# A decoder trunk on one core: the final sum as products with diagonal matrices, queries by halves of the tokens, output weights loaded during the merge

## The reference, cut to what matters

```python
x = layer_norm(x_in)                                  # D_MODEL = 1024
z = x @ w_in + b_in                                   # nine streams of 512 columns, four gates of 1024
mix = (sum over 4 branches of sigmoid(gate) * (branch @ w_branch)) @ w_out      # the merge, then w_out
x = layer_norm(ALPHA * x + mix)
x = layer_norm(ALPHA * x + cross_attend(x, mem))      # queries x @ x_wq, 4 heads, 256 memory rows, then @ x_wo
s = sigmoid(x @ router_w)                             # 16 experts; the best group of 4, the best 2 experts in it
h = silu(x @ e_wg[e]) * (x @ e_wu[e])                 # each expert on the tokens that chose it
y = sum over the two chosen experts of w[e] * (h @ e_wd[e])
out = layer_norm(ALPHA * x + y)
```

## Time and profile before

| what | value |
|---|---|
| runs | median 1628.93 us of 3 (1626.19 to 1635.36) |
| profiled execution: own time, span | 1631.28 us, 1629.5 us |
| PE busy | 1403.6 us (86%) |
| DVE, ACT, POOL busy | 752.3 us (46%), 538.4 us (33%), 239.5 us (15%) |
| mean granted TensorE clock | 0.938 of full speed |
| chain of waits, by engine | PE 37%, DMA 7%, DVE 4%, ACT 2%, SP's queue 2%, issue 2% |

### The profile page before, as it was taken

The page is one execution under the profiler, slowest core; times in us unless marked ns, Lnnn a source line. Parts: engine busy times, 40 slices in busy tenths (PEclk is TensorE's granted clock), DMA queues, the critical chain, the costliest instruction groups (busy, mean ns, idle before and its releaser), DMA issues.

```text
span 1629.5 us, 18477 instructions
## 1 busy us (share of the span) xinstructions
PE 1403.6 (86%) x7275; PEld 1166.8 (72%) x7275; DVE 752.3 (46%) x1079; ACT 538.4 (33%) x729; POOL 239.5 (15%) x211
## 2 busy tenths in 40 slices
PE   4989989899896688899999798987896799999940
PEld 4767868677685576798999686775684588887730
DVE  5024133242425546753111143032345699888847
ACT  1234421424312033421000001144201488777721
POOL 4200000000005422132333000001000110010023
PEclk9999999999997899999999998999997799999985
DMA  9613332331002222124222603126802699999941
GB/s 323 229 48 104 97 99 78 86 97 39 16 0 58 59 59 59 39 78 129 78 78 87 224 0 103 52 100 249 283 33 97 214 378 395 394 394 394 394 176 66
DMA packets 175091, 239.84 MB, mean 147 GB/s; under 512 B 6048, under 2 KB 108633, under 8 KB 174881
## 3 DMA queue, kind: packets, MB, share of 16 engines
q1 hardware_dynamic: 156896, 181.13, 32.9%
q0 software_dynamic: 14832, 52.57, 9.1%
q10 hardware_dynamic: 3281, 5.00, 1.0%
HBM read 214.08 MB, written 24.60 MB: 146 GB/s over the span
## 4 chain that ended last, share of the span: by engine, by line
PE 37%; DMA 7%; DVE 4%; ACT 2%; SPq 2%; issue 2%; POOL 0%; DVEq 0%; POOLq 0%; ACTq 0%
PE bank L1034 35%; DMA expert_weights<-in_e_wg_dram 3%; SPq L672 1%; DMA kv_k<-in_cache_mem_k_dram 1%; DVE x_tok L2114 1%; DMA ring<-in_w_out_dram 1%; ACT kv_t L718 1%; DVE small L1545 1%; SPq L661 1%; PE bank L1455 1%; ACT x_tok L1025 0%; DMA xg<-x_scratch,table 0%; DVE x_tok L2109 0%; DMA yb<-expert_rows,ints 0%; ACT xgT_hi L997 0%
## 5 line engine op out<-in xcount | busy, mean ns | idle before, releaser
L1034 PE MATMUL bank<-xT,ring 128*128 128x288 f32 x1152 | 297.2, 419 | 0.9 <-ACT xT L718 0.9
L1034 PEld LDWEIGHTS bank<-xT,ring 128*128 128x128 f32 x1152 | 223.9, 197 | 65.0 <-issue 1.7
L1903 DVE TENSOR_TENSOR expert_weights_lo<-expert_weights,expert_weights_hi 128x2048 fp32r<-128x2048 f32 x96 | 217.8, 2288 | 39.4 <-ACT expert_weights_hi L955 39.1
L955 ACT ACTIVATE expert_weights_hi<-expert_weights 128x2048 fp32r<-128x2048 f32 x96 | 183.4, 1917 | 50.3 <-DMA expert_weights<-in_e_wg_dram 22.8
L1034 PE MATMUL bank<-x_hi,gate_weights_hi 128*128 128x288 f32 x512 | 167.3, 327 | 14.7 <-DVE ob L1694 11.9
L1034 PE MATMUL bank<-x_lo,gate_weights_hi 128*128 128x288 f32 x512 | 154.4, 302 | 0.0
L1034 PE MATMUL bank<-x_hi,gate_weights_lo 128*128 128x288 f32 x512 | 154.2, 301 | 0.0
L1034 PE MATMUL bank<-ob,branch_weights 128*128 128x288 f32 (+1 forms) x512 | 134.5, 405 | 0.0
L866 ACT ACTIVATE gate<-bank,pc 128x288 f32<-128x288 f32 x64 | 31.8, 501 | 270.6 <-PE bank L1034 263.8
L1034 PEld LDWEIGHTS bank<-x_hi,gate_weights_hi 128*128 128x128 f32 x512 | 100.5, 196 | 18.7 <-DVE ob L1694 12.0
L1034 PE MATMUL bank<-expert_weights_hi,xgT_hi 128*128 128x512 f32 x256 | 103.1, 403 | 7.4 <-DVE xgT_lo L2081 7.4
(11 more groups left out here) (393 smaller groups left out, 2136.7 us busy)
## 6 DMA issues: line engine op xcount, KB each, us to landing
expert_weights<-in_e_wg_dram SPq DMA_DIRECT2D x32, 1024.0 KB, 13.6
expert_weights<-in_e_wu_dram SPq DMA_DIRECT2D x32, 1024.0 KB, 14.5
expert_weights<-in_e_wd_dram SPq DMA_DIRECT2D x32, 1024.0 KB, 14.1
gate_weights<-in_w_in_dram SPq DMA_DIRECT2D x32, 512.0 KB, 3.9
ring<-in_w_in_dram SPq DMA_DIRECT2D x24, 512.0 KB, 6.5
branch_weights<-in_w_branch_dram SPq DMA_DIRECT2D x32, 256.0 KB, 3.2
kv_k<-in_cache_mem_k_dram POOLq DMA_DIRECT2D x8, 1024.0 KB, 7.3
kv_v<-in_cache_mem_v_dram POOLq DMA_DIRECT2D x8, 1024.0 KB, 5.5
```

Of the source, the lines that this page charges most:

```text
L955: act.activation(w_hi[n % HIS][:], w_raw[n % RAW][:], ACT.Copy).then_inc(w_hi_done, 1)
L1034: return pe.matmul(out, lhsT, rhs, start=start, stop=stop)
L1903: dve.tensor_tensor(w_lo[n % RAW][:], w_raw[n % RAW][:], w_hi[n % HIS][:].bitcast(F32), ALU.subtract).then_inc(w_lo_done, 1)
```

## The change

The diff has five parts.

1. **Output weights.** wo1 to wo3 get places of their own (`wo_rest`), outside the ring, and ACT issues them in the step `states`, ahead of the reload of `x_tok`. SP loads the query and attention output weights in the order wq0, wq1, wq2, wx0, wx1, wq3, wx2, wx3; wq3 takes the slot of wo0.
2. **Queries by halves.** The units go over all four chunks for the first half of the tokens and then for the second. PE turns tile t-1 after the mix of tile t, and the last tile after the second query unit. The norm after the mix goes tile by tile.
3. **Norms in two operations.** (x - mean) * g before the wait for the root, then times the reciprocal, plus b.
4. **Positions in one pass.** The chosen flags and the two constants of "pos" become fp32r. One comparison and one sum replace four DVE operations. ACT runs a sigmoid on one column before the router's scores arrive. `weights_lo(3)` moves from behind the table's copy to the end of the router's work on DVE.
5. **The end.** Eleven 128x128 diagonal matrices (ALPHA, and each token's two weights by tile) are made on DVE during the first five experts, in place of the scaling of `x_tok`. PE sums the final row of a tile in PSUM: three products per half of 512 columns. The gathers of the earlier experts' rows start when expert 14's rows are stored, those of the later rows when expert 15's are; PE makes both earlier terms of tiles 0 to 3 before it waits for the first later row. DVE takes the statistics and applies the norm from PSUM; ACT only takes the root, and POOL only gathers.

```diff
-            n = first_merge + 1
-            for w in (w_out, x_wq, x_wo):
-                for c in range(1 if w is w_out else 0, 4):
-                    load(n, [(slot_k8(chunks[n][1]), w1024(w, c))])
+            for n in [first_merge + k for k in (4, 5, 6, 8, 9, 7, 10, 11)]:
+                name, slot, _, _ = chunks[n]
+                load(n, [(slot_k8(slot), w1024(x_wq if name[:2] == "wq" else x_wo, int(name[2])))])
...
                     act.wait_ge(sgu_done, KW)
+                    for c in range(1, 4):
+                        slot = chunk[f"wo{c}"][0]
+                        act.dma_start(slot_k8(slot), w1024(w_out, c)).then_inc(landed[slot], 16)
...
+def query_units():
+    return [(c, 2 * m + half) for half in range(2) for c in range(4) for m in range(2)]
...
             for t in range(NT):
                 token_major("mix", mer, "wo", t)
-            for t in range(NT):
-                turn_tokens("yT", x_tok, t, ln_out, NT + t + 1)
+                if t:
+                    turn_tokens("yT", x_tok, t - 1, ln_out, NT + t)
+            for c, n in query_units():
+                if (c, n) == (1, 0):
+                    turn_tokens("yT", x_tok, NT - 1, ln_out, 2 * NT)
...
             def norm_apply(n, x, g, b, rows, done):
                 o = 16 * (n % 2)
+                dve.scalar_tensor_tensor(x, x, small[0:rows, o + 12:o + 13], g[0:rows], ALU.subtract, ALU.mult)
                 dve.wait_ge(ln_std, n + 1)
                 link(dve.reciprocal(small[0:rows, o + 14:o + 15], small[0:rows, o + 15:o + 16]))
-                link(dve.tensor_scalar(x, x, small[0:rows, o + 12:o + 13], small[0:rows, o + 14:o + 15],
-                                       ALU.subtract, ALU.mult))
-                link(dve.tensor_tensor(x, x, g[0:rows], ALU.mult))
-                dve.tensor_tensor(x, x, b[0:rows], ALU.add).then_inc(done, 1)
+                dve.scalar_tensor_tensor(x, x, small[0:rows, o + 14:o + 15], b[0:rows], ALU.mult, ALU.add).then_inc(done, 1)
...
-            mm(ps[:, 0:NE * (NT + 1)], cst[:, C_STRI:C_STRI + P], chosen_and_zero, True, False)
+            mm(ps[:, 0:NE * (NT + 1)], count_cst[:, 0, :], chosen_r[:], True, False)
...
-            link(dve.tensor_scalar(tiles, count, float(P), None, ALU.is_gt))
-            for k in range(2, NT):
-                link(dve.scalar_tensor_tensor(tiles, count, float(P * k), tiles, ALU.is_gt, ALU.add))
+            link(dve.tensor_tensor(over, count.unsqueeze(2).to_broadcast([P, NE, NT - 1]),
+                                   tile_starts[:, 1:NT].unsqueeze(1).to_broadcast([P, NE, NT - 1]), ALU.is_gt))
+            link(dve.tensor_reduce(tiles, over, AX, ALU.add))
...
+            act.activation(small[:, 36:37], small[:, 33:34], ACT.Sigmoid)
             act.wait_ge(rt_logit, 1)
...
             dve.tensor_copy(table[:, 0:MOE_T], ps[:, 0:MOE_T]).then_inc(fr, 1)
-            weights_lo(3)
...
+            weights_lo(3)
             dve.wait_ge(x2_stored, 16 * NT)
...
+            def scaled(t, s, n, rows_of_pair, start, stop):
+                rows = TILES[t]
+                return mm(bank[sum_banks[t][s]][0:rows, :], pair_diag[0:rows, n, 0:rows],
+                          rows_of_pair[0:rows, 512 * s:512 * s + 512], start, stop)
+            def earlier_terms(t):
+                if t == 3:
+                    released(f"eY{NE - 1}")
+                    released(f"eY'{NE - 1}")
+                if t == 4:
+                    pe.wait_ge(sum_free, 1)
+                pe.wait_ge(yb_landed[t], 16)
+                for s in range(2):
+                    scaled(t, s, 0, x_tok[:, t, :], True, False)
+                    scaled(t, s, 2 + 2 * t, yb[t][:], False, False)
+            for t in range(NT - 1):
+                earlier_terms(t)
+            for t in range(NT):
+                if t == NT - 1:
+                    earlier_terms(t)
+                pe.wait_ge(ya_landed[t], 16)
+                for s in range(2):
+                    scaled(t, s, 1 + 2 * t, ya[:, t, :], False, True).then_inc(sum_full, 1)
...
+                    for s in range(2):
+                        dve.wait_ge(sum_full, 2 * t + s + 1)
+                        link(dve.bn_stats(small[0:rows, o + 6 * s:o + 6 * s + 6], bank[sum_banks[t][s]][0:rows, :]))
...
+                        ins = dve.scalar_tensor_tensor(x[:, half], bank[sum_banks[t - 1][s]][0:rows, :], small[0:rows, o + 12:o + 13],
+                                                       lng[0:rows, half], ALU.subtract, ALU.mult)
+                    ins.then_inc(sum_free, 1)
...
+                    dve.scalar_tensor_tensor(x, x, small[0:rows, o + 14:o + 15], lnb[0:rows], ALU.mult, ALU.add).then_inc(last_written, 1)
...
+            pool.wait_ge(ys_stored[0], 16 * (NE // 2))
+            pool.wait_ge(ys_stored[1], 16 * (NE // 2 - 1))
+            for t in range(NT):
+                gather_pairs(t, yb[t], 2, ys_d[0:P * (NE - 1)]).then_inc(yb_landed[t], 16)
             used = tiles_used(pool)
...
+            pool.wait_ge(ys_stored[1], 16 * (NE // 2))
             for t in range(NT):
+                gather_pairs(t, ya[:, t, :], 0, ys_d).then_inc(ya_landed[t], 16)
```

More of the change, by code:

```diff
@@ L128, in psum_schedule @@
         high(f"yT{t}b")
-    for c in range(4):
-        for n in range(4):
-            low(f"q{c}{n}")
+    for c, n in query_units():
+        low(f"q{c}{n}")
     for n in range(4):
@@ L314, in weight_plan @@
     before = len(plan)
+    slots = [n % RING for n in range(before)]
     plan += [(f"wo{c}", 1, f"mix{NT - 1}{'ab'[c // 2]}") for c in range(4)]
@@ L317, in weight_plan @@
     plan += [(f"wx{c}", 1, f"att{NT - 1}{'ab'[c // 2]}") for c in range(4)]
-    landed, out = [0] * RING, []
-    for n, (name, dmas, last) in enumerate(plan):
-        landed[n % RING] += 16 * dmas
-        out.append((name, n % RING, landed[n % RING], last))
+    slots += [2, RING, RING + 1, RING + 2, 0, 1, 3, 2, 4, 5, 0, 1]
+    landed, occupant, out = [0] * (RING + 3), {}, []
+    for (name, dmas, last), slot in zip(plan, slots):
+        landed[slot] += 16 * dmas
+        out.append((name, slot, landed[slot], occupant.get(slot)))
+        occupant[slot] = last
     return out, before, landed
@@ L394, in trunk @@
         h0 = place("h0", 53132, [P, KW, NSEQ])
+        wo_rest = [place(f"mixer_output_weights{k + 1}", at, [P, SLOT]) for k, at in enumerate((48064, 50112, 40640))]
         mem_tok = place("mem_tok", 16896, [P, 2, D])
@@ L440, in trunk @@
         ya = place("ya", 0, [P, NT, D])
-        yb = place("yb", 5120, [P, NT, D])
+        yb = [place(f"yb{t}", 31744 + D * t if t < NT - 1 else 48064, [P, D]) for t in range(NT)]
+        pair_diag = place("pair_diag", 29184, [P, 1 + 2 * NT, P])
         rsc = place("rsc", 40640, [P, 17, NT * NE])
@@ L465, in trunk @@
         passed = sem("loop_wait_passed")
-        landed = [sem(f"ring{k}_landed") for k in range(RING)]
+        landed = [sem(f"ring{k}_landed") for k in range(RING)] + [sem(f"mixer_output_weights{k}_landed") for k in range(1, 4)]
         def acquire(eng, name):
@@ L594, in slot_free @@
             def slot_free(n):
-                if n >= RING:
-                    last = chunks[n - RING][3]
-                    b, use = uses[last]
+                if chunks[n][3]:
+                    b, use = uses[chunks[n][3]]
                     sp.wait_ge(full[b], use + 1)
@@ L959, in turned_out @@
                     copy_out(f"zT{t}{'ab'[s]}", xT[:, 4 * s:4 * s + 4, t * P:t * P + TILES[t]], (0, 4 * TILES[t]))
+            act.activation(count_cst[:, 0, :], cst[:, C_STRI:C_STRI + P], ACT.Copy)
+            act.activation(count_cst[:, 1, :], cst[:, C_ONE:C_ONE + P], ACT.Copy).then_inc(count_ready, 1)
             weights_hi(0)
@@ L1019, in _ @@
             for t in range(NT):
-                n, rows = n_ln + 2 * NT + t, TILES[t]
-                o = 16 * (n % 2)
-                deviation(n, rows)
-                x = x_tok[0:rows, t, :]
-                act.wait_ge(last_mean, t + 1)
-                act.activation(x, x, ACT.Identity, bias=small[0:rows, o + 11:o + 12],
-                               scale=small[0:rows, o + 14:o + 15]).then_inc(last_normed, 1)
+                deviation(n_ln + 2 * NT + t, TILES[t])
         @block.tensor
@@ L1898, in _ @@
             dve.wait_ge(ld_rows, 112)
-            norm_tiles(tile_of, lng, lnb, ln_out, lambda t: residual("mix", t))
+            for t in range(NT):
+                residual("mix", t)
+                norm_stats(tile_of(t), TILES[t])
+                norm_apply(n_ln[0] - 1, tile_of(t), lng, lnb, TILES[t], ln_out)
             def weights_lo(n):
@@ L2301, in _, with gather_pairs @@
                     gather(n + 2, n % 2).then_inc(xg_landed[n % 2], 16)
+            def gather_pairs(t, y, k, source):
+                rows = TILES[t]
+                return pool.indirect_dma_start(y[0:rows, :], None, source, bass.IndirectOffsetOnAxis(ap=ints[0:rows, k, t:t + 1], axis=0))
+            pool.wait_ge(rt_slots, 1)
```

(4 more changed lines are left out.)

125 lines of the change are left out of this document (65 added, 60 removed).

## The result

The changed kernel took 1602.15 us (median of 4 runs, 1599.52 to 1603.86), the kernel before 1629.38 us on the same chip (4 runs, 1626.19 to 1635.36). The ratio is 0.9832, 95% interval 0.9815 to 0.9849: 27 us faster. The forecast was 38 us faster, 1591.2 us, with a range of 1585 to 1604. The sign and the range held. Three stages came out 17.0 us worse than forecast (10.6, 3.3 and 3.1 us), and the others 8.2 us better, 3.4 us of that in two stages that the change does not touch. That the range held is in part luck.

A forecast was written before the change was run, and what follows sets the result against it. PE, busy 86% of the span, was taken to bound the kernel; gains of 9.0 + 8.4 + 0.8 + 5.0 + 14.5 = 37.7 us took the profiled 1631.28 us to 1593.6, so 1591.2 us for the median, range 1585 to 1604.

The forecast's parts named there:

- Output weights: Output product: weights loaded during the merge remove PE's 6.5 us wait and 2.5 us of half-rate loss; gain 9.0 us.
- those land some 4 us ahead of need, so I cost it at nothing, with 2 us as the other end: Merge: gate weight loads sharing DMA engines with the 3 MB prefetch were expected to cost nothing, at most 2 us.
- my signs of being wrong: Listed: late gate weights, PE waiting for earlier rows beyond 1573, diagonal records of 0.87 us, or a grown expert stage.
- the prefetch gives nothing: Rival, merge: the three loads hold up gate weights by as much as they save; total 1600.2 us, chance 6%.
- Queries by halves: Between output product and queries: 6.7 us of thin work and 1.7 us of half-rate start go; gain 8.4 us.
- Norms: Spatial norms and first norm: three DVE operations become two; gain 0.8 us in all, ends 0 and 2.
- Router: Scores to first gather: norm, early sigmoid, position products, fewer DVE operations and moved weights_lo(3); gain 5.0 us.
- the moved operation: Router: weights_lo(3) behind the short operations lets the first gather out 1.85 us earlier, ends 0 and 1.9.
- positions and counts: Router: fewer position product records win 0.6 us, and four small DVE operations becoming two win 0.3 us.
- the norm and the table load: Router: last tile's shorter norm wins 1.0 us; the early sigmoid hides the activation table load, 1.3 us.
- The end: After PE's last expert product: final rows summed on PE, norm on DVE; new end 1615.0, gain 14.5 us.
- The rival of half rate through the end: Rival, end: PE runs the final products at half rate, losing 5 us there; total 1610.7 us, chance 6%.
- that rival: Rival, expert stage: the 23.2 us won ahead are lost if something else times the weight stream; 1614.4 us, 5%.

The follow-up runs named there:

- run 1: Changed kernel without prefetch: the three output weight loads go back to SP's queue behind the merge's loop; 1603.48 us, ratio 0.9853.
- run 3: Changed kernel with only the first norm back in its old three operations; 1598.2 us, ratio 0.9817.
- run 5: Changed kernel with x_tok reloaded behind the merge's loop and the first norm in its old three operations; 1590.76 us, ratio 0.9763.
- run 9: Changed kernel with late x_tok reload and 8 thrown-away products in PE's wait for the second weight chunk; 1597.55 us, ratio 0.9794.
- run 12: Changed kernel with the three output weight loads issued by ACT behind its last gate activation of the loop, and the old first norm; 1603.27 us, ratio 0.9848.
- run 2: Changed kernel with the x_tok reload moved behind ACT's last gate activation of the merge's loop, weights still prefetched; 1592.24 us, ratio 0.9781.
- run 6: Changed kernel with late x_tok reload and 16 thrown-away products in PE's wait for the second weight chunk; 1601.22 us, ratio 0.9823.
- run 10: Changed kernel with late x_tok reload, the same kernel as run 2 measured once more for its attention; 1595.52 us (one run).
- run 11: Changed kernel with the three output weight loads issued by ACT behind its last gate activation of the loop; 1606.79 us, ratio 0.9872.
- run 7: Changed kernel with each prefetched output weight load fetching an eighth of its rows, so the result differs; 1592.12 us (one run), loop 166.21 us.

## Why the prediction was right and where it was wrong

**Output weights: the step that failed.** The 9.0 us in the output product were right (9.3, run 1). Wrong was "those land some 4 us ahead of need, so I cost it at nothing, with 2 us as the other end". The cost was 10.6 us. I compared the gate load's lead of 4 us with nothing: the step left out how long the engines need for all that is in flight, 5.25 MB at some 370 GB/s, near 15 us, and that small packets share the engines one for one with large ones. Gate weights late after the loop's start were among my signs of being wrong. The rival "the prefetch gives nothing" had the mechanism and the time (1600.2 us), and I gave it 6%. My evidence against it, that the reload of `x_tok` had that place without a wait, was a load of 2.25 MB; with 3 MB more ahead of it the same place is another one. ACT's delay was mis-sized on the same ground: its gate activation came at 757.71, not 752.7, of which 2.5 us are the loop's later start. The rest is issuing, which took longer with the weight loads ahead in the queue (1.05 us a reload in place of 0.71).

**Queries by halves:** 8.4 forecast, 9.1 measured (18.4 less 9.3). Right, the clock part included.

**Norms:** 0.8 us of gain forecast for the first and the spatial ones; the loop starts 2.5 us later in the changed kernel's profile, 1.7 on the average of the eight profiles with this start. The step looked at DVE alone. An engine that starts earlier runs sooner into the next wait, 4.93 us for the second chunk in place of 0.67, and in the changed kernel's profile the clock was at 0.50 from 30 to 36. Runs 3, 5, 9 and 12 bear it out in the loop's start; how much is the clock and how much the landing of the chunk is not separated.

**Router:** 5.0 us forecast, 1.9 measured. Its lines after, against the earlier trace rows:

```profile
1231.16 3.40 PE L1050 MATMUL bank<-rw,xT 128*128 128x16 f32 x16 [1.27 <-ACT xT L726]
...
1236.04 1.28 ACT L989 ACT_TABLE_LOAD   x1
...
1243.64 1.56 PE L1050 MATMUL bank<-chosen_r,count_constants 128*128 128x96 f32 x6 [5.61 <-DVE chosen_r L2043]
...
1255.54 1.04 POOL L2348 DMA_INDIRECT xg<-x_scratch,table  x1 [21.18 <-DVE table L2083]
```

The end of the gather's first issue gained 3.3 us against the start of the router: 1.8 from the moved operation (forecast 1.85), 1.1 from positions and counts (0.9), but 0.4 from the norm and the table load, where 2.3 were forecast. The norm of the last tile was ready earlier, and PE was not: it was in the fourth tile's scores, at half clock for longer, 3.40 us in place of 2.57 (line below, kernel before), and the transposes queued behind. In run 1, with another course of the clock, these two gave 1.9 us and the router 3.7. Then 1.1 us went in the first expert's products, which ran at half rate longer.

```profile
1238.09 2.57 PE L1034 MATMUL bank<-rw,xT 128*128 128x16 f32 x16 [1.27 <-ACT xT L718]
```

**The end:** 14.5 forecast, 18.3 measured. The order was right, and the gain was larger because three durations were taken too long. Store and first gather took 2.65 and 4.42 us in place of 3.71 and 5.6 (2.2 us), the granted clock stayed at 1.00 where I had added 1.5 us for a fall (PE was idle for 0.90 us, not 3.0), and DVE needed 22.3 us, not 23.5; 0.9 us went again, since I had counted one of the first tile's two later products. The rival of half rate through the end was wrong.

Nothing was lost in the experts; that rival was wrong too.

**What stays open.** Why the clock falls in the attention. Its stage took 99.75 to 109.24 us in the profiles of this study; the falls in its middle came in runs 2, 5, 6, 9, 10 and 12 and not in the others. In runs 1 and 11 the clock fell once some 13 us into the stage. Neither the late x_tok (run 12 has none) nor a stretch before it with next to no waits (run 7) decides. That is as large as most of what was tested here, so the profile's stages, not the sums, carry the verdicts on edits under 5 us.

## What to carry to other kernels

Before moving a load into a stage, add the bytes that will be in flight beside it and divide by the rate the windows show; compare that with the lead of the smallest load that a tight loop waits for, not with that load's usual landing. Look at the size of the packets too: beside a load in large packets, one in small packets got as many turns here, and so a small part of the bytes. Two bulk transfers with different due times don't belong in one burst: moving the one needed last gave the whole gain back. An earlier start is worth something only up to the next wait.

## What the hardware showed that I had not expected

- A 512 KB load took 16.0 us to be of use while 5.25 MB were in flight from another engine's queue, and 7.5 us with 3 MB.
- Two queues at work side by side moved 474 and 476 packets in 5 us, but 1.70 and 0.24 MB; three moved 653 or 654 each in 10 us, 2.54, 0.67 and 0.65 MB.
- A transfer's issue took longer behind more bytes: five reloads took ACT 3.50 us behind 0.375 MB and 5.23 us behind 3 MB.
- Of three loads issued 2.1 us earlier, but on a queue of their own, the last was there 2.8 us later than where they stood ahead of the following loads in one queue.
- Equal work and equal waits of 2.4 us were followed by a granted clock of 1.00 in one kernel and 0.58 in another.
